# A hybrid decoder layer on one core: another order of the retention chunks, an earlier load of values, and sample tiles packed as one block

## The reference, cut to what matters

```
z   = rmsnorm(x) @ w_in                     # 1024 -> 7 x 512: rq rk rv rg aq ak av
ro  = groupnorm(retention(rope(rq), rope(rk), rv)) * silu(rg)    # 8 heads of 64
ao  = merge of dilated softmax attention over aq, ak, av         # 8 heads of 64
x   = x + rmsnorm(concat(ro, ao) @ w_out)
x   = x + rmsnorm((silu(gate) * up) @ w_down),  gate, up = rmsnorm(x) @ w_gu
```

```
inner = (q k^T) * decay;   o = inner v + (q S) * cross_decay;   S = S * g^C + (k * k_decay)^T v
```

## Time and profile before

| | us |
|---|---|
| median of 3 runs (range) | 1695.41 (1694.04 to 1699.86) |
| profiled execution | 1691.11 |
| its span | 1689.5 |
| TensorE busy in the span | 1581.5 (94%) |
| VectorE, ScalarE, GpSimd busy | 609.5, 405.8, 384.4 |
| input projection, first to last matmul | 0 to 371.7 |
| retention | 375.8 to 477.6 |
| prompt attention | 477.6 to 636.9 |
| sample attention | 636.9 to 757.4 |
| output projection | 757.4 to 876.0 |
| feed-forward | 876.0 to 1689.5 |

### The profile page before, as it was taken

One profiled execution on the slowest core, in us unless ns is written; L12 is line 12 of the kernel. 1 busy time (PEld: TensorE's weight loads), 2 busy tenths in 40 slices (PEclk: granted clock), 3 DMA queues, 4 the chain that ended last, 5 costly groups with the idle time before them and its releaser, 6 DMA issues.

```text
span 1689.5 us, 23363 instructions
## 1 busy us (share of the span) xinstructions
PE 1581.5 (94%) x9366; PEld 1369.9 (81%) x9366; DVE 609.5 (36%) x977; ACT 405.8 (24%) x720; POOL 384.4 (23%) x459
## 2 busy tenths in 40 slices
PE   7999999988878888879999999999999999999994
PEld 6788888878745556657889999999999999999983
DVE  2233110105666654433552233333323233332355
ACT  4300121211134544442332111211111111111121
POOL 3254300013322223002554111111111111111111
PEclk9999999998779999989999999999999999999997
DMA  6323334119163109954335654545455354653445
GB/s 210 117 72 122 124 124 160 47 67 323 53 208 114 51 13 362 414 215 115 113 94 188 168 141 128 153 111 161 128 144 153 106 168 116 154 149 113 130 113 166
DMA packets 120272, 245.29 MB, mean 145 GB/s; under 512 B 20652, under 2 KB 82364, under 8 KB 115045
## 3 DMA queue, kind: packets, MB, share of 16 engines
q1 hardware_dynamic: 111400, 157.15, 29.6%
q0 software_dynamic: 6976, 71.32, 14.7%
q10 hardware_dynamic: 1824, 15.83, 2.3%
HBM read 214.08 MB, written 106.21 MB: 190 GB/s over the span
## 4 chain that ended last, share of the span: by engine, by line
PE 52%; DVE 1%; DMA 1%; issue 0%; POOL 0%; ACT 0%; DVEq 0%; POOLq 0%
PE y_ps L2126 30%; PE x_ps L2140 7%; PE y_ps L1730 6%; PE m_ps L2140 4%; PE d_ps L2140 4%; DMA own<-x_mid_scratch 1%; PE x_ps L1777 0%; DVE acc L2057 0%; DVE acc L2061 0%; PE m_ps L1724 0%; POOL stat L1936 0%; DVE acc L2045 0%; DVE m_lo L1676 0%; ACT m_hi L1637 0%; PE y_ps L2181 0%
## 5 line engine op out<-in xcount | busy, mean ns | idle before, releaser
L2126 PE MATMUL y_ps<-h_hi,gu_hi 128*128 128x384 f32 (+1 forms) x1056 | 345.9, 328 | 0.0
L2126 PE MATMUL y_ps<-h_hi,gu_lo 128*128 128x384 f32 (+1 forms) x1056 | 345.5, 327 | 0.0
L2126 PE MATMUL y_ps<-h_lo,gu_hi 128*128 128x384 f32 (+1 forms) x1056 | 345.4, 327 | 0.0
L2126 PEld LDWEIGHTS y_ps<-h_hi,gu_hi 128*128 128x128 f32 x1056 | 198.2, 188 | 2.0
L2126 PEld LDWEIGHTS y_ps<-h_lo,gu_hi 128*128 128x128 f32 x1056 | 198.2, 188 | 2.0
L2126 PEld LDWEIGHTS y_ps<-h_hi,gu_lo 128*128 128x128 f32 x1056 | 198.2, 188 | 0.0
L1904 POOL TENSOR_TENSOR f<-silu,f 128x384 fp32r<-128x384 f32 (+1 forms) x66 | 60.6, 918 | 604.5 <-ACT f L1966 422.4
L478 PE MATMUL z_ps<-w_hi,h_hi 128*128 128x512 f32 x488 | 191.3, 392 | 4.3 <-POOL h_lo L331 4.3
L478 PE MATMUL z_ps<-w_lo,h_hi 128*128 128x512 f32 x488 | 190.6, 391 | 0.0
L478 PE MATMUL z_ps<-w_hi,h_lo 128*128 128x512 f32 x488 | 190.4, 390 | 0.0
L2037 DVE TENSOR_TENSOR silu<-silu,y_ps 128x384 f32<-128x384 f32 (+1 forms) x66 | 35.1, 532 | 357.9 <-ACT silu L1963 352.4
(11 more groups left out here) (236 smaller groups left out, 2238.9 us busy)
## 6 DMA issues: line engine op xcount, KB each, us to landing
ks_sample<-cache_k_win POOLq DMA_DIRECT2D x60, 544.0 KB, 6.5
vs_sample<-cache_v_win POOLq DMA_DIRECT2D x60, 544.0 KB, 7.8
raw<-w_gu SPq DMA_DIRECT2D x84, 256.0 KB, 7.0
K<-cache_k_win SPq DMA_DIRECT2D x8, 2048.0 KB
w_raw<-w_in SPq DMA_DIRECT2D x14, 1024.0 KB
z_scratch<-z_out SPq DMA_DIRECT2D x56, 256.0 KB, 2.0
raw<-w_down SPq DMA_DIRECT2D x22, 512.0 KB, 5.5
zr<-z_scratch SPq DMA_DIRECT2D x8, 1024.0 KB, 10.3
```

Of the source, the lines that this page charges most:

```text
L2126: mm = pe.matmul(bank[u % 2][:, 0:n], w[s][:, k, h, :], x[:, k, c:c + n], start=(k, m) == (0, 0), stop=(k, m) == (KT - 1, 2))
```

## The change

*Retention.* TensorE's scores go one chunk ahead, its transposes two:

```diff
 turn(0)
+inner(0)
+turn(1)
+update(0)
 for t in range(PT):
-    inner(t)
-    update(t)
-    turn(t + 1)
+    inner(t + 1)
     output(t)
-inner(SAMPLE)
+    if t + 2 < TT:
+        turn(t + 2)
+    if t + 1 < PT:
+        update(t + 1)
```

VectorE's centring comes one chunk later, its gate two; `oc` has two buffers, GpSimd multiplies in place, `on` is gone:

```diff
 for t in range(PT):
     scores(t)
+    if t:
+        centre(t - 1)
     if t + 1 < PT:
         carry(t + 1)
     if t == 2:
         tables.build_rows(dve)
     if t:
         variance(t - 1)
-        finish(t - 1)
-    centre(t)
-last_state()
+    if t >= 2:
+        finish(t - 2)
 scores(SAMPLE)
 sample_queries()
+centre(PT - 1)
+last_state()
 variance(PT - 1)
+finish(PT - 2)
 one_sequence(dve, slice(0, DEC_B // 2 + 1))
 finish(PT - 1)
...
-if t:
-    dve.wait_ge(on_ready, t)
-dve.tensor_tensor(oc[0:rows], o_ps[t % 2][0:rows], ...)
+if t >= 2:
+    dve.wait_ge(mix_ready, t - 1)
+dve.tensor_tensor(oc[0:rows, t % 2], o_ps[t % 2][0:rows], ...)
...
-if t:
-    pool.wait_ge(mix_ready, t)
-pool.tensor_tensor(on[0:rows], oc[0:rows], ...)
+pool.tensor_tensor(oc[0:rows, t % 2], oc[0:rows, t % 2], ...)
```

*Both projections.* The 64 low rows and the 64 high rows of the sample tile form one block of 128, which is multiplied by the high and by the low weights: two matmuls for each k in place of three. The two halves of the PSUM tile are then added. In the input projection:

```diff
+terms = ((h_hi, w_hi), (h_hi, w_lo), (h_lo, w_hi))[:3 if t < PT else 2]
 for k in range(KT):
-    for n, (x, w) in enumerate(((h_hi, w_hi), (h_hi, w_lo), (h_lo, w_hi))):
-        mm = pe.matmul(z_ps[t % 3][:, :], x[:, k, end - 128:end], w[:, par, k, :], ...)
+    for n, (x, w) in enumerate(terms):
+        mm = pe.matmul(z_ps[t % 3][:, :], x[:, k, t * 128:t * 128 + 128], w[:, par, k, :], ...)
...
+def take_low(k):                                   # ScalarE
+    n = at(k, PT)
+    act.wait_ge(z_done, n + 1)
+    if k > 0:
+        act.wait_ge(z_evac, at(k - 1, PT) + 1)
+    act.copy(sums[NS:128, :], z_ps[n % 3][0:NS, :]).then_inc(sample_low, 1)
...
+def fold(k):                                       # VectorE
+    dve.wait_ge(sample_low, k + 1)
+    dve.tensor_tensor(sums[NS:128, :], z_ps[at(k, PT) % 3][NS:128, :], sums[NS:128, :],
+                      ALU.add).then_inc(folded, 1)
```

`evacuate` and `rotate` of the sample tile wait for `folded` and read `sums`. GpSimd's low part of the sample tile goes into `h_hi` beside the high one. The output projection does the same with `m_hi` (the low part into its columns 64 to 127, two terms in `products`):

```diff
+n, src = tile_rows(t), self.y_ps[t % 2]
+if t == PT:
+    act.copy(self.sums[0:NS, :], src[NS:128, :]).then_inc(self.sample_low, 1)
+    act.wait_ge(self.folded, 1)
+    src = self.sums
-act.activation(self.y[:, :], self.y_ps[t % 2][:, :], ACT.Square, ...)
+act.activation(self.y[0:n, :], src[0:n, :], ACT.Square, ...)
...
+if t == PT:                                        # VectorE
+    dve.wait_ge(self.sample_low, 1)
+    dve.tensor_tensor(self.sums[0:NS, :], src[0:NS, :], self.sums[0:NS, :], ALU.add).then_inc(self.folded, 1)
+    dve.wait_ge(self.folded, 1)
```

*Values of sequence 1.* Their buffer moves to an address that overlaps the first six heads of the prompt's bias, which are done with when the last pair begins. SP asks for them in the prompt attention, before the store of the last pair; GpSimd clears the padding there:

```diff
 if p == 1:
     second_keys(sp)
+if p == NPAIR - 1:
+    second_values(sp)                              # sp.wait_ge(padded, 4); load_values(..., 1)
 sp.wait_ge(O_ready, 4 * p + 4)
...
 pool.wait_ge(share_ready, g + 1)
+if g == PT * (NPAIR - 1):
+    clear_second(pool)
...
 def _(sp):                                         # sample attention
-    sp.wait_ge(set_up, 2)
-    load_values(sp, A, z, V, V_landed, 1)
     out.load_weights(sp, 0, out.w_a)
```

More of the change, by code:

```diff
@@ L444, in _ @@
                         mean(t)
+                fold(0)
                 dve.wait_ge(rstd_ready, TT)
@@ L452, in _ @@
                     for t in range(TT):
+                        if t == PT:
+                            fold(k)
                         if k in ROTATED:
@@ L473, in project @@
                         pe.wait_ge(z_evac, TT * c + t - 2)
-                    end = t * 128 + tile_rows(t)
-                    first, last = (0, 0), (KT - 1, 2)
+                    terms = ((h_hi, w_hi), (h_hi, w_lo), (h_lo, w_hi))[:3 if t < PT else 2]
+                    first, last = (0, 0), (KT - 1, len(terms) - 1)
                     for k in range(KT):
-                        for n, (x, w) in enumerate(((h_hi, w_hi), (h_hi, w_lo), (h_lo, w_hi))):
-                            mm = pe.matmul(z_ps[t % 3][:, :], x[:, k, end - 128:end], w[:, par, k, :],
+                        for n, (x, w) in enumerate(terms):
+                            mm = pe.matmul(z_ps[t % 3][:, :], x[:, k, t * 128:t * 128 + 128], w[:, par, k, :],
                                            start=(k, n) == first, stop=(k, n) == last)
@@ L794, in finish @@
                         dve.wait_ge(mix_stored[t % 2], 16 * (t // 2))
-                    dve.tensor_tensor(mixr[0:rows, t % 2, :], on[0:rows].rearrange("p h d -> p (h d)"), head(t, 3, 0, NH),
+                    dve.tensor_tensor(mixr[0:rows, t % 2, :], oc[0:rows, t % 2].rearrange("p h d -> p (h d)"), head(t, 3, 0, NH),
                                       ALU.mult).then_inc(mix_ready, 1)
@@ L930, in __call__, with prompt_attention @@
         return self.nc.alloc_sbuf_tensor_at(name, shape, dtype, offset=here)
-def prompt_attention(nc, A, z, mix_t, bias, ident, q_n, k_n, qk_landed, clear, ahead, second_keys, spare, retained):
+def prompt_attention(nc, A, z, mix_t, bias, ident, q_n, k_n, qk_landed, clear, ahead, second_keys, clear_second, second_values, spare, retained):
     UNITS, LAST = NPAIR * PT, NPAIR * PT - 1
@@ L2251, in hymba_layer @@
         w_b = K[:, 0, 0:2 * HELD, :].rearrange("p (k a) c -> p k (a c)", a=2)
-        with nc.sbuf_tensor("out_inputs", [128, (Layout.W_B - Layout.W_A) // 4], F32):
-            sample_attention(nc, A, z, mix_t, bias_s, ident, K, V, q_s, K_landed, V_landed, q_landed, out, w_b)
+        with nc.sbuf_tensor("out_inputs", [128, (VALUES_AT + VALUES - nc.sbuf_base) // 4], F32):
+            sample_attention(nc, A, z, mix_t, bias_s, ident, K, (V, V_second), q_s, K_landed, V_landed, q_landed, out, w_b)
         with_3_4.close()
```

103 lines of the change are left out of this document (67 added, 36 removed).

## The result

The changed kernel takes 1676.05 us (median), the kernel before 1694.72 beside it: ratio 0.9886, 95% interval 0.9869 to 0.9903. That is a gain of 1.1%, clear of the noise and in the direction that was forecast, and inside the range (1650 to 1677), but 15 us above the forecast of 1661: 18.7 us gained in place of 34.3. The profiled execution has a span of 1674.0 us (before 1689.5), 15.5 less.

What follows compares the result with a forecast made beforehand. TensorE bounds the input and output projections, VectorE's wait for GpSimd retention, transfers the sample attention. Gains 11.3 + 18.7 + 2.3 + 2.0 = 34.3 us take the profiled 1691.1 to 1656.8; with 4.3 for the median, 1661; range 1650 to 1677.

Steps and rivals of the forecast that it cites:

- Part 1: Input projection: 16 matmuls in place of 24 for the sample tile in seven groups, one fold uncovered; 11.3 us gained.
- Part 2: Retention: reordered chunks overlap, TensorE becomes the bound at 6.15 us a chunk in place of 9.04; 18.7 us gained.
- The tail: End of retention: from the sample mask to the centring of the sample output, 13.0 us with hand-overs.
- Rival A: Retention: GpSimd takes the shared SBUF port pair first, VectorE waits 1.64 us a chunk; 7 us less gained, 1668; chance 0.18.
- Part 3: Sample attention: sequence 1's values load earlier, in the prompt attention, so later keys come sooner; 2.3 us gained.
- 0.88 MB / 378 GB/s = 2.3 us: Sample attention: only 0.88 MB still stood ahead of keys 3, so moving the values away saves 2.3 us.
- Part 4: Output projection: 16 of the last tile's 48 matmuls go, but the transposes wait for `xn`; 2.0 us gained.
- The feed-forward stage keeps its time.: Feed-forward: this stage was taken to be unchanged, a difference of 0.

Runs made afterwards that it cites:

- a_rows_last: The changed kernel with the output projection's rows loaded behind all keys and the second half of the output weights: 1668.08 us, ratio 0.9822 to the kernel before.
- b_val: The kernel before with only the earlier load of sequence 1's values added: 1699.39 us, ratio 1.0007.
- a_rows_late: The changed kernel with the output projection's rows loaded with the keys of sequences 6 and 7, not 4 and 5: 1676.50 us, ratio 0.9892 to the kernel before.
- a_build4: The changed kernel with the table's rows built on VectorE in the fifth retention chunk, not the third: 1669.09 us, ratio 0.9855 to the kernel before.

## Why the prediction was right and where it was wrong

The time lies inside the range by luck in part: its upper end, 1677, was set for a retention that gives 5 us. Retention gave 15.7, and it was 10.8 us that the forecast had put nowhere that brought the time there.

**Part 1 was right,** step and size: 11.15 us of 11.3 (over the runs the projection ends at 363.0 to 366.5 with this part, at 375.8 to 377.6 without it). At the end the copy and the add stand 360.53 - 359.19 = 1.34 us ahead of the evacuation, and nothing covers them (forecast 1.4):

```profile
359.19 0.58 ACT L365 COPY sums<-z_ps 64x512 f32<-64x512 f32 x1 [2.94 <-PE z_ps L511]
360.53 0.72 ACT L385 ACTIVATE z_out<-sums,stat 64x512 f32<-64x512 f32 x1 [0.76 <-DVE sums L429]
```
```profile
359.80 0.69 DVE L429 TENSOR_TENSOR sums<-z_ps,sums 64x512 f32<-64x512 f32 x1 [46.45 <-ACT sums L365]
```

**Part 2 was right in its mechanism:** chunks of 6.02 us where nothing else held them up (6.15 forecast), the clock up, TensorE and ScalarE as the bound. What failed is the sum of seven such chunks: with the two waits shown above they took 48.3 us and not 43.05. The tail was shorter than thought: from the sample mask to the centring of the sample output are 435.59 - 424.93 = 10.7 us, not 13.0.

```profile
435.59 0.67 DVE L807 TENSOR_REDUCE stat<-o_ps 64x8 f32<-64x512 f32 x1
```

So the trace after gave 15.7 of 18.7. Over the runs the new order took 84.4 us on average (nine runs), the old one 104.7 (five), a difference of 20. Rival A had the right resource and the wrong loser: VectorE began 0.17 us before GpSimd, so GpSimd's power was stretched to 2.02, in a chunk where it has time. The forecast had missed that the landing of a constant, 0.7 us late in the trace before, can hold up the faster pipeline (1.0 to 4.8 us in six runs).

**Part 3 was wrong.** The step that failed is "0.88 MB / 378 GB/s = 2.3 us", with the sentence before it that transfers are the limit from there on. I counted bytes in one stream. There are two queues: values on ScalarE's, keys and rows on SyncE's. From 628.0 to 684.5 us 408 GB/s moved 23.1 MB. That is about what had been asked for by then: four loads of keys (3 to 6) and 2.1 MB of rows on the one queue, 12.7 MB, and four loads of values (2 to 5) on the other, 10.6. The profile has 12.46 MB on SyncE's queue (q1) and 10.53 on ScalarE's (q10) in this window, so each got about half. The Trainium skill (DMA: Bandwidth & Descriptors, section "Queues, rings and completion order") says that a DMA engine goes round between the queues that have work, a packet at a time; the trace agrees with its near half and half. A load of keys ahead of which rows stand is thus paid at about half rate, while values arrive that nobody needs yet. That the order and not the sum decides is shown by a_rows_last: the same bytes, 113.65 us.

So the early values did not bring their 2.3 us. Of the 2.64 MB taken from the head, most was lost in the hole: 25 us into the stage SyncE's queue had moved 8.95 MB before and 6.79 after, a lead of 0.5 MB. Keys 4 did come almost in time (the third step is 13.7 us, before 18.1, without a wait 12.65; some 2.7 us late was the forecast), but the wait went on to keys 5. For ScalarE asks for the values of sequence 5 when it has scaled the output of 3, and with keys 4 on time that is 59.9 us into the stage and not 64.3, while keys 5 are still due:

```profile
701.20 0.33 ACTq L1208 DMA_DIRECT2D V_second<-cache_v_win  x1
```
```profile
668.65 0.33 ACTq L1253 DMA_DIRECT2D V_second<-cache_v_win  x1
```

From 60 to 70 us into the stage SyncE's queue (q1) moved 3.64 MB before and 2.13 after (packets, MB, share):

```profile
q1 hardware_dynamic: 366, 3.64, 87.4%
```
```profile
q1 hardware_dynamic: 273, 2.13, 51.9%
```

The 3.8 us that this pair lost are no measure: the stage took 117.6 to 124.1 us, on average 120.4, in five traces with the old loads, and 121.6 on average in the four with the early values and the rows in their first place. b_val, the part by itself, is at 1.0007 of the kernel before (at most 2.2 us gained).

**Part 4 was right:** 1.9 of 2.0, and the transposes stand right behind `xn`, which ends at 846.82 + 1.75 = 848.57:

```profile
846.82 1.75 DVE L1760 TENSOR_SCALAR xn<-xm,stat 128x1024 f32<-128x1024 f32 x1 [0.67 <-POOL stat L1660]
...
848.62 1.09 PE L1835 MATMUL x_ps<-ident,xn 128*128 128x128 f32 x8 [1.47 <-DVE xn L1760]
```

Alone it can't be told from no change (0.9991).

**The largest miss is a sentence without a number: "The feed-forward stage keeps its time."** It lost 10.8 us, over half of what was missing, and none of the rivals had it. What the runs show in its place: 40 matmul instructions fewer ahead of the loop moved its code to where every pass fetches it anew (27 to 28 packets more over three jumps back, 9 a pass), and each jump costs a pause of 1.3 to 1.9 us. Two of the three cost 1.6 us more at the low clock: 5.5 + 3.2 = 8.7 of the 10.8. The rest I did not trace; stages without pauses differ by 2.3 us among themselves (812.7 to 815.0). In a_rows_late and a_build4 the clock stayed at 1.00 behind all three pauses (5.2 and 4.9 us in all), and the stage took 819.4 and 819.3: so the place of the loop costs 5 to 11 us here. Both directions were shown by shifting alone. Why just this place is bad was not measured; 0, 16 and 24 matmuls fewer are good places, 40 is not. The Trainium skill (Runtime: NRT & Kernel Launch, section "Instruction fetch mechanics") gives TensorE 128 KB of instruction memory, filled in blocks of 16 KB, and warns of jumps whose target isn't there. The packet of 16 KB agrees. An estimate from the Trainium skill's 128 KB and the 9 packets: if a pass lies in 8 blocks, which are all there is room for, and one more is fetched ahead, the first is gone at the jump. No run shows that this is the reason. The Trainium skill's narrower statement in the same section, that only two blocks are within reach, does not fit the kernel before, to which one packet came in 400 us of its loop.

## What to carry to other kernels

An instruction taken out moves all code behind it: where the profile has a long loop, compare the instruction queue's packets and the "issue" waits at its jumps before and after, and if they grew, shift the program by a few idle instructions where the engine waits anyway. Where two queues feed one consumer, count bytes per queue, at about half the rate each (12.46 and 10.53 MB here), and in the order in which they are needed; put loads that nobody needs soon behind all those that somebody waits for. And look at a stage's transfers for holes before crediting a moved load with its bytes: time freed while no buffer is free was worth nothing here.

## What the runs showed of the hardware that was not expected

- A loop of TensorE that runs some 143 us a pass either stays on the chip (one packet in 400 us) or is fetched in every pass (9 of 16 KB), depending on some tens of instructions ahead of it; a jump costs 1.3 to 1.9 us of pause, and behind some pauses (two of three in the trace after, none in a_rows_late) come 3.2 us at 0.51 of the clock.
- A semaphore increment on TensorE's queue took 0.153 us (6.1, 13.4 and 28.1 us for 32, 80 and 176).
- A VectorE operation on 8 columns, with one SBUF input, took 2.74 us beside a GpSimd operation of 2.74 that had begun 0.03 us before it, where 0.17 is usual.
